# An encoder step in fp32 halves: the seam between the attention part and the MLP is laid out in another order

## The reference

```python
def _layer(x, ...):
    h = _rmsnorm(x, g_mix)
    q_m, k_m, v_m, o_m, i_pre, f_pre, q_a, k_a, v_a = _split_cols(h @ w_in)
    h_til, c1, n1, m1 = _mlstm_chunkwise(qm, km, vm, i_pre + b_igate, f_pre + b_fgate, c0, n0, m0, chunk)
    h_m = jax.nn.sigmoid(o_m) * _rmsnorm(h_til, g_head...)
    o_a = _swa_attention(qb, kb, vb, q_pos, k_pos, attn_sinks)
    x = x + jnp.concatenate([h_m, o_a], axis=-1) @ w_out
    x = x + jnp.square(jax.nn.relu(_rmsnorm(x, g_mlp) @ w_up)) @ w_down
    x = x + jax.nn.sigmoid(_rmsnorm(x, g_ple) @ w_ple_gate) * (p @ w_ple_proj)
```

## Time and profile before

| | us |
|---|---|
| median of 3 runs (lowest, highest) | 2599.46 (2599.33, 2600.07) |
| the profiled execution, its time | 2600.81 |
| its span in the profile | 2599.2 |
| PE busy | 2558.8 |
| DVE busy | 1884.8 |
| ACT busy | 905.1 |
| POOL busy | 78.7 |

### The profile page before, as it was taken

One profiled execution on the slowest core, in us unless ns is written; L12 is line 12 of the kernel. 1 busy time (PEld: TensorE's weight loads), 2 busy tenths in 40 slices (PEclk: granted clock), 3 DMA queues, 4 the chain that ended last, 5 costly groups with the idle time before them and its releaser, 6 DMA issues.

```text
span 2599.2 us, 40780 instructions
## 1 busy us (share of the span) xinstructions
PE 2558.8 (98%) x14143; PEld 2224.1 (86%) x14143; DVE 1884.8 (73%) x3281; ACT 905.1 (35%) x2097; POOL 78.7 (3%) x170
## 2 busy tenths in 40 slices
PE   8999999999999999999999999999999999999999
PEld 6888888878888878999999888989888888888887
DVE  7777777775555568777777788888887887885443
ACT  5333333454444443222222323232332332343322
POOL 0000000000000000000000000000000000000010
PEclk9999999999999999999999999999999999999999
DMA  5112111542232336222222542323342222233223
GB/s 211 58 57 85 56 56 51 178 156 98 105 109 97 112 129 236 65 65 65 65 65 65 196 136 65 97 65 97 121 156 81 65 80 65 81 142 135 86 73 108
DMA packets 163367, 261.86 MB, mean 101 GB/s; under 512 B 11440, under 2 KB 111256, under 8 KB 162520
## 3 DMA queue, kind: packets, MB, share of 16 engines
q1 hardware_dynamic: 160936, 252.29, 28.9%
q0 software_dynamic: 2352, 8.52, 1.0%
HBM read 199.99 MB, written 60.62 MB: 100 GB/s over the span
## 4 chain that ended last, share of the span: by engine, by line
PE 89%; DVE 6%; issue 2%; ACT 1%; DMA 1%; POOL 0%; ACTq 0%; DVEq 0%; SPq 0%; POOLq 0%
PE m_proj L112 12%; PE m_proj L114 12%; PE m_proj L113 12%; PE m_turned L112 6%; PE m_turned L114 6%; PE m_turned L113 6%; PE m_acc L114 5%; PE m_acc L112 5%; PE m_acc L113 5%; PE m_pair L113 4%; PE m_pair L112 4%; PE m_pair L114 4%; PE m_pair L1260 1%; PE m_turned L1268 1%; PE m_acc L1285 1%
## 5 line engine op out<-in xcount | busy, mean ns | idle before, releaser
L2082 ACT ACTIVATE f_up_hi<-f_sums 128x512 fp32r<-128x512 f32 x138 | 85.8, 621 | 507.1 <-DVE f_sums L2365 489.8
L2396 DVE TENSOR_TENSOR f_part<-f_part,m_acc 128x384 f32<-128x384 f32 (+2 forms) x240 | 119.2, 513 | 139.9 <-PE m_acc L114 137.1
L112 PE MATMUL m_proj<-f_down_hi,f_uT_hi 128*128 128x512 f32 x476 | 188.9, 397 | 2.5 <-DVE f_acc L2439 2.5
L114 PE MATMUL m_proj<-f_down_hi,f_uT_lo 128*128 128x512 f32 x476 | 185.6, 390 | 0.0
L112 PE MATMUL m_turned<-f_down_hi,f_uT_hi 128*128 128x512 f32 x472 | 183.9, 390 | 1.6 <-DVE f_acc L2431 0.9
L113 PE MATMUL m_proj<-f_down_lo,f_uT_hi 128*128 128x512 f32 x476 | 185.2, 389 | 0.0
L113 PE MATMUL m_turned<-f_down_lo,f_uT_hi 128*128 128x512 f32 x472 | 184.1, 390 | 0.0
L114 PE MATMUL m_turned<-f_down_hi,f_uT_lo 128*128 128x512 f32 x472 | 183.9, 390 | 0.0
L2439 DVE TENSOR_TENSOR f_acc<-f_acc,m_proj 128x1024 f32<-128x1024 f32 x118 | 143.7, 1218 | 45.4 <-PE m_proj L114 45.2
L2439 DVE TENSOR_TENSOR f_acc<-f_acc,m_turned 128x1024 f32<-128x1024 f32 x131 | 151.5, 1156 | 27.6 <-PE m_turned L114 25.5
L2106 ACT ACTIVATE f_uT_hi<-f_part 128x256 fp32r<-128x256 f32 (+2 forms) x300 | 92.3, 364 | 202.0 <-PE m_turned L114 122.2
(11 more groups left out here) (452 smaller groups left out, 7324.8 us busy)
## 6 DMA issues: line engine op xcount, KB each, us to landing
f_down_raw<-in_w_down SPq DMA_DIRECT2D x96, 512.0 KB, 5.1
f_up_raw<-in_w_up SPq DMA_DIRECT2D x92, 512.0 KB, 5.2
hT_hi_kept<-m_hT_hi SPq DMA_DIRECT2D x17, 512.0 KB, 5.0
hT_lo_kept<-m_hT_lo SPq DMA_DIRECT2D x17, 512.0 KB, 5.8
a_hT_hi<-hT_hi_kept SPq DMA_DIRECT2D x17, 512.0 KB, 3.7
a_hT_lo<-hT_lo_kept SPq DMA_DIRECT2D x17, 512.0 KB, 4.6
m_x<-in_x_prompt SPq DMA_DIRECT2D x16, 512.0 KB, 4.2
a_x_sum<-in_x_prompt SPq DMA_DIRECT2D x16, 512.0 KB, 6.2
```

The source lines that it names most:

```text
L112: eng.matmul(out, lh(k), rh(k), start=f, stop=False)
L114: ins = eng.matmul(out, ll(k), rh(k), start=False, stop=e)
L2082: act.activation(up_hi[:, q], weight(q), ACT.Copy).then_inc(up_hi_made, 1)
L2396: dve.tensor_tensor(part[out][:, 0:w], part[other][:, 0:w], up_ps[bank][:, 0:w], ALU.add).then_inc(combined, 1)
```

## The change

- **SP**: block 0's up weights are loaded behind the stores of round 16's K and V (mark "kept") and not at the end of round 16.
- **DVE and ACT, weights**: the sums and the first low part go into round 16 (mark "split"), three more low parts behind the second softening of round 17, the last three behind the decode tile's shares (mark "shared").
- **Operands**: on DVE the five of a unit (B11, T1, T3, B22, T2) are made as one chain each; unit 0's chain goes ahead of tile 15's second add. Then come unit 0's low T2, the chains of units 1 and 2 and their low T2s, then round 18 of attention (scaling of tile 15, the decode tile's adds), then the nine low parts of T3, T1, B21, then the T4s. ACT has the same order in HI_EARLY, HI_NEXT, HI_LATE, and comes back to attention's round 18 (its copy of tile 15's `hxT`) behind the last T4. The operands have other places in memory (FIRST_PLACE).
- **Decode tile on PE**: its mLSTM heads are turned in round 17 between the halves of the tile 15 product, ACT copies them there, and four of eight chunks of its high product are done ahead of the average. Tile 15's `turn_x` goes behind the third of the seven first up products.
- **PE, every round from 2 to 17**: the second scores go ahead of the wait for the low mixed operand and of `turn_x`.
- **POOL**: unit 2's rows are loaded ahead of tile 15's root.

```diff
@@ -960,7 +960,6 @@
     EARLY = 2
-    FRONT, BACK = 2, 6
@@ -1062,6 +1061,8 @@
                 sp.dma_start(out_v[which][P - rows:P, :], kv[0:rows, slot, KVW:]).then_inc(kept_out, 16)
+            if on_round(r, NT):
+                yield "kept"
             if exists(r - 2):
@@ -1168,8 +1169,9 @@
                 act.activation(mixT_to[:, HEADS:KC, 0:old.n], outT[slot][:, :, 0:old.n], ACT.Copy).then_inc(mix_hi, 1)
-                all_of(act, mix_turned, old.i)
-                act.activation(mixT_to[:, 0:HEADS, 0:old.n], turned[:, 0:HEADS, 0:old.n], ACT.Copy).then_inc(mix_hi, 1)
+                if not on_round(r, NT + 2):
+                    all_of(act, mix_turned, old.i)
+                    act.activation(mixT_hi[:, 0:HEADS, :], turned[:, 0:HEADS, :], ACT.Copy).then_inc(mix_hi, 1)
             if on_round(r, NT + 1):
@@ -1186,6 +1188,8 @@
                 if on_round(r, NT + 1):
+                    all_of(act, mix_turned, NT)
+                    act.activation(mixT_dec[:, 0:HEADS, :], turned[:, 0:HEADS, 0:DEC], ACT.Copy).then_inc(mix_hi, 1)
                     yield "free"
@@ -1195,6 +1199,8 @@
                     act.activation(q_parts[rows, :, b, 0:cur.n], turned[rows, 0:GRP, 0:cur.n], ACT.Copy).then_inc(qk_rounded, 1)
+                if on_round(r, NT):
+                    yield "split"
             if on_round(r, 1):
@@ -1323,8 +1329,13 @@
                     pe.wait_ge(*m.heads_done)
+                if on_round(r, NT + 2):
+                    reached(pe, mix_hi, NT * 2 + 1)
+                    reached(pe, added, (NT - 1) * 2 + 1)
+                    project_last_out(wo_hi, range(HEADS))
                 average(old)
-                turn_heads(old)
+                if not on_round(r, NT + 2):
+                    turn_heads(old)
             if exists(cur.i):
@@ -1333,24 +1344,23 @@
                 project_kv(cur)
+            if exists(mid.i) and not on_round(r, 1):
+                score(mid, 1)
             if on_round(r, NT + 2):
                 all_of(pe, mix_hi, old.i, 2)
-                project_last_out(wo_hi, range(FRONT)).then_inc(o0_ps, 1)
-            elif exists(old.i):
+                project_last_out(wo_hi, range(HEADS, KC)).then_inc(o0_ps, 1)
+                project_last_out(wo_lo, range(1)).then_inc(o0_ps, 1)
+                project_last_out(wo_lo, range(1, KC)).then_inc(o1_ps, 1)
+                yield "out"
+                turn_x(done)
+                yield r
+                return
+            if exists(old.i):
                 all_of(pe, mix_lo, old.i, 2)
...
                 turn_x(done)
-            if exists(mid.i) and not on_round(r, 1):
-                score(mid, 1)
             if on_round(r, 2):
                 pe.wait_ge(wo_lo_made, HALF)
-            if on_round(r, NT + 2):
-                project_last_out(wo_hi, range(FRONT, BACK)).then_inc(o0_ps, 1)
-                project_last_out(wo_hi, range(BACK, KC))
-                project_last_out(wo_lo, range(1)).then_inc(o0_ps, 1)
-                project_last_out(wo_lo, range(1, KC)).then_inc(o1_ps, 1)
-                yield r
-                return
             if exists(old.i):
@@ -1362,6 +1372,9 @@
                 project_out(0, second).then_inc(o0_ps, 1)
+                if on_round(r, NT + 1):
+                    reached(pe, sT_sb, NT * 2 + 1)
+                    turn_heads(mid)
                 all_of(pe, kv_sb, r if exists(r) else NT)
@@ -1375,7 +1388,7 @@
                 else:
-                    reached(pe, sT_sb, mid.i * 2 + 1)
+                    reached(pe, mix_hi, NT * 2 + 1)
                 turn_s(mid, 1)
@@ -1480,8 +1493,6 @@
                 split_mix(old)
-            if on_round(r, NT + 2):
-                yield "mixed"
             if exists(cur.i) and not on_round(r, 0):
@@ -1507,6 +1518,8 @@
                 share(mid, 1)
+                if on_round(r, NT + 1):
+                    yield "shared"
             if exists(cur.i):
@@ -1530,8 +1545,8 @@
-    finished = Finished(scaled=(x_scaled, NT + 1), q_ps=(q_ps, NT + 1), kv_ps=(kv_ps, NT + 1), front_ps=(o0_ps, NT + 1), out_ps=(o1_ps, NT + 1), x_out=(x_out, 16 * (NT + 1)), hxT_out=hxT_out, kept_out=(kept_out, 96),
-                        middle_ps=(o0_ps, NT + 2), back_ps=(o0_ps, NT + 3), mix_ps=(o1_ps, NT), soft=(soft, (NT * 2 + 1) * SOFT + 1))
+    finished = Finished(scaled=(x_scaled, NT + 1), q_ps=(q_ps, NT + 1), kv_ps=(kv_ps, NT + 1), front_ps=(out_done, NT + 1), out_ps=(o1_ps, NT + 1), x_out=(x_out, 16 * (NT + 1)), hxT_out=hxT_out, kept_out=(kept_out, 96),
+                        middle_ps=(o0_ps, NT + 1), back_ps=(o0_ps, NT + 2), mix_ps=(o1_ps, NT), soft=(soft, (NT * 2 + 1) * SOFT + 1))
     return Programs(sync, gpsimd, scalar, tensor, vector), finished
@@ -1559,7 +1574,7 @@
             whole(m)
-            upto(a, NT)
+            upto(a, "kept")
             next(f)
@@ -1575,7 +1590,7 @@
             next(f)
-            upto(a, NT + 2)
+            upto(a, NT + 1)
             next(f)
@@ -1593,6 +1608,8 @@
             whole(m)
+            upto(a, "split")
+            next(f)
             upto(a, "free")
@@ -1611,7 +1628,7 @@
             whole(m)
-            upto(a, NT + 2)
+            upto(a, "out")
             upto(f, "drained")
@@ -1637,11 +1654,13 @@
             whole(m)
+            upto(a, "split")
+            next(f)
             upto(a, "free")
             next(f)
+            upto(a, "shared")
+            next(f)
             upto(a, "idle")
-            next(f)
-            upto(a, "mixed")
             next(f)
@@ -1919,13 +1938,13 @@
         if p == 0:
-            return by_pair(by_unit[:, u, lo, which])
+            return by_pair(by_unit[:, u, lo, FIRST_PLACE[which]])
         return by_pair(by_pass[p][lo][:, which, :, unit_cols(p, u)])
...
             return by_pass[p][lo][:, q, c, :]
-        return by_unit[:, :, lo, q, c, :]
+        return by_unit[:, :, lo, FIRST_PLACE[q], c, :]
@@ -1937,13 +1956,13 @@
-    STAGED_FIRST = [(0, T1), (0, T3), (0, T2), (0, T4), (1, T1), (1, T3), (1, T2), (2, T1), (2, T3), (2, T2), (1, T4), (2, T4)]
-    HI_EARLY = [(0, B11), (0, B22), (0, B21), (0, T2), (0, T3)]
-    HI_BY_STAGE = [(1, B11), (1, B22), (2, B11), (2, B22), (1, T2), (2, T2), (1, T3), (2, T3), (0, T1), (1, T1), (2, T1),
-                   (1, B21), (2, B21), (0, T4), (1, T4), (2, T4)]
-    HI_FIRST = HI_EARLY + HI_BY_STAGE
-    LO_FIRST = [(0, B11), (0, B22), (0, B21), (0, T2), (0, T3), (1, B11), (1, B22), (2, B11), (2, B22), (1, T2), (2, T2), (1, T3), (2, T3),
-                (0, T1), (1, T1), (2, T1), (1, B21), (2, B21), (0, T4), (1, T4), (2, T4)]
+    STAGED_FIRST = [(0, T1), (0, T3), (0, T2), (1, T1), (1, T3), (1, T2), (2, T1), (2, T3), (2, T2), (0, T4), (1, T4), (2, T4)]
+    HI_EARLY = [(0, B11), (0, B22)]
+    HI_NEXT = [(0, T2), (1, B11), (1, B22), (2, B11), (2, B22), (1, T2), (2, T2)]
+    HI_LATE = [(0, T3), (1, T3), (2, T3), (0, T1), (1, T1), (2, T1), (0, B21), (1, B21), (2, B21), (0, T4), (1, T4), (2, T4)]
+    HI_FIRST = HI_EARLY + HI_NEXT + HI_LATE
+    LO_FIRST = [(0, B11), (0, B22), (0, T2), (1, B11), (1, B22), (2, B11), (2, B22), (1, T2), (2, T2)] + HI_LATE
+    FIRST_PLACE = {T3: 0, B11: 1, B22: 2, T2: 3, T1: 4, B21: 5, T4: 6}
@@ -2133,19 +2152,23 @@
-        whole(ready(0, 0))
+        weights = ready(0, 0)
+        next(weights)
+        next(weights)
+        yield
+        whole(weights)
         act.wait_ge(*a.soft)
-        first_hi(*HI_EARLY[0])
-        yield
-        for u, which in HI_EARLY[1:]:
+        for u, which in HI_EARLY:
             first_hi(u, which)
...
         act.wait_ge(*a.front_ps)
-        for u, which in HI_BY_STAGE:
-            if (u, which) == (2, B11):
-                act.wait_ge(*a.middle_ps)
+        for u, which in HI_NEXT:
             first_hi(u, which)
+        act.wait_ge(*a.middle_ps)
+        for u, which in HI_LATE:
+            first_hi(u, which)
+        yield
         for p in PASSES:
@@ -2219,6 +2242,8 @@
             for q, out in enumerate(out_all):
+                if q == 3:
+                    upto(rest, NT + 2)
                 if q == 6:
@@ -2507,35 +2532,37 @@
-        add_weights(0)
-        whole(ready(0, 0))
-        yield
-        first_lo(0, B11)
-        first_stage(0, T1)
-        first_stage(0, T3)
-        yield
-        first_lo(0, B22)
-        first_stage(0, T2)
-        first_lo(0, B21)
-        first_stage(0, T4)
-        first_lo(0, T2)
-        first_lo(0, T3)
-        for u in (1, 2):
-            if u == 2:
-                dve.wait_ge(*a.back_ps)
+        def first_chain(u):
             first_lo(u, B11)
...
             first_stage(u, T2)
-        for u, which in LO_FIRST[9:16]:
+
+        weights = ready(0, 0)
+        add_weights(0)
+        next(weights)
+        yield
+        for _ in range(3):
+            next(weights)
+        yield
+        whole(weights)
+        first_chain(0)
+        yield
+        first_lo(0, T2)
+        first_chain(1)
+        dve.wait_ge(*a.middle_ps)
```

(14 more changed lines are left out.)

## The result

The changed kernel took 2618.37 us (median of 4 runs, 2618.11 to 2618.72), the kernel before, beside it on the same chip, 2599.39 (4 runs, 2597.90 to 2600.07): a ratio of 1.0075 [1.0063, 1.0087], 19.0 us slower.

What follows compares the result with a forecast made beforehand. PE, busy 98% of the span, was taken as the bound. Block 1's later start of 14.65 us plus 1.5 for the clock gave +16.1, added to the median 2599.46: 2615.6 us, range 2608 to 2621.

Steps and rivals of the forecast that it cites:

- The deciding step: SP, round 18: held until ACT's row copy at 986.4, so second up weights land at 1007.7; block 1 14.65 us later.
- the queue: DMA, before block 1: POOL's four pass 1 loads delay the second up weights by 4.0 us, of 0 to 5.1.
- sign that the queues slow each other: Tile 16's 128 KB store, issued at 989.13 with POOL's loads close behind, took 10.2 us; read as queues slowing each other.
- Rival (a): Same wait of SP, but POOL's loads cost nothing: +12.2 us, 2611.6; chance 0.20.
- Rival (b): Same wait, with 5.1 for the queue, 3.0 for the clock, 1.5 for down weights: +20.2, 2619.7; chance 0.12.
- The clock term: PE, start of block 1: restarts at the lower clock after over 10 us idle, losing 1.5 us, of 1.1 to 3.0.
- The steady rounds: PE, every round: second scores moved ahead of the low mixed operand's wait and turn_x; 0, between -0.5 and +0.5 us.
- The lead at the first product: PE, round 18: first up product starts near 974 to 975 instead of 979.67, 5 us ahead.
- The full clock at 948: PE, round 17: scores cut the 1.89 us gap to 0.9, so PE stays at full clock.
- The reason given for the lost lead: ACT takes P1 behind the T4s, so PE stands from 983.3 to 986.9; DVE's chain is only 1.8 to 2.1 ahead.
- rival (d): First operands ready 5 to 5.6 us sooner and lead kept, with P1 and row copy on time: 2594.0; chance 0.04.
- Rival (c): No change: second weights land before DVE reaches them near 990.9; block 1 starts some 2.1 earlier, 2597.3; chance 0.07.

Runs made afterwards that it cites:

- Experiment 1: Changed kernel, but SP passes its mark "loads" ahead of the store of tile 15's rows in round 18; 2598.74 us, ratio 1.0000.
- experiment 2: Kernel before, with one added SP wait for the 21st high operand ahead of the first up weights' stores; 2616.43 us, ratio 1.0068.
- experiment 3: Changed kernel, but POOL's four loads for pass 1 wait until the second up weights have landed; 2613.31 us, ratio 1.0057.
- experiment 4: Experiment 1 with the second scores of rounds 2 to 16 behind turn_x again, round 17's still moved; 2598.42 us, ratio 0.9999.
- experiment 6: Kernel before with only the early load, sums and first parts of the first up weights in round 16; 2598.57 us, ratio 0.9996.
- Experiment 7: Experiment 5 with ACT's three high T4s moved behind its copy of tile 15's rows and P1; 2596.80 us, ratio 0.9993.
- experiment 5: Experiment 1 with ACT making the third and fourth high up weights ahead of the decode tile's heads; 2598.18 us, ratio 0.9997.
- experiment 8: Experiment 7 with unit 0's high T2 ahead of the square of tile 15 on ACT; 2596.88 us, ratio 0.9993.
- experiment 9: Experiment 7's kernel run again, unchanged, for more runs; 2597.92 us, ratio 0.9995.

## Why the prediction was right, and where it was off

**The deciding step** held, with its place and its cause: SP's program stands at tile 15's rows, behind it the first weights' stores and the second weights' loads. The store came at 986.69 (foreseen: the copy ends at 986.4; it did at 986.66), the load landed at 1009.7 (1007.7). Experiment 1 takes the wait away and the loss goes; experiment 2 makes it alone and the loss comes. Together they leave no room for another cause of more than a microsecond or two. (Experiment 2's spans differ by 14.2 and not 17.7; its sums start 3.4 sooner than after's, which accounts for it.)

**The size** was 1.6 us short of the spans' difference (+16.1 for +17.7): 1.7 from one term of the sum, the queue, 0.4 ahead of the seam and 0.5 the other way from the clock, and the last two are within what traces differ by. Against the medians the forecast of 2615.6 was 2.8 short of 2618.37. The other 1.2 are the base: I added a difference to before's profiled execution to a median that lies 1.35 below it. That execution holds the 1.7 us of the clock at 948, so against the 66.81 without that fall the seam lost 18.0.

I took 4.0 for the queue, of 0 to 5.1, the upper end being POOL's bytes at the rate of the earlier trace rows. It was 5.7 as after stands to before (23.0 - 17.3), and 6.1 with POOL's loads taken away (experiment 3), over the upper end that I had worked out. The rate of the best microsecond was no bound. From the end of the copy to the first sum, after moved 8.27 MB in 23.1 us, a mean of 358 GB/s, and experiment 3 5.90 MB in 17.0, 348 GB/s. By 358 the 2.1 MB are 5.9 us. The difference is 2.37 MB: 2.10 of POOL's queue and 0.26 more of SP's own.

The prediction's sign that the queues slow each other, the 10.2 us of tile 16's store of 128 KB, was misread. Six loads of acc tiles stood right ahead of it on SP's own queue:

```profile
981.08 7.57 SPq L1970 DMA_DIRECT2D f_acc<-x_after_mixers  x6
```

In after the same store, issued at 1007.56 behind the same six loads, took as long, and from 1007.5 to 1017.7 POOL's queue moved nothing:

```profile
x_after_mixers<-a_x_sum SPq DMA_DIRECT2D x1, 128.0 KB, 10.1
```

In experiment 1, where it is issued 6 us after the last of the six loads and POOL's loads come 1.8 us behind it, it took 4.2. So the choice of 4.0 rested in part on a wrong sign, and that it came near is partly luck; experiment 3 is what shows that POOL's loads cost the weights time.

Rival (a), no cost of the queue, falls with experiment 3. Rival (b), 2619.7, was nearer to the measured time (1.3 over) than the forecast (2.8 under). Its queue term was nearer, but 3.0 for the clock is not borne out, and PE has no further gap behind 1013.19 that before lacks, so the down weights cost 0.
The Trainium skill (DMA: Bandwidth & Descriptors, Queues, rings and completion order) has each DMA engine take turns between the queues by packets; the prediction said that by this rule the charge lies near the upper end, and experiment 3 agrees with 6.1 us.

**The clock term** was 1.5 of 1.1 to 3.0, and what stands behind the first sum grew by 1.0. Whether that is under the range can't be told: the three kernels with a late block 1 have 1607.05 to 1608.15 there, the other eight 1605.30 to 1607.16, and their means differ by 1.4. PE ran at 1.2 GHz for 5.4 us behind the restart; at full loss that would be 2.7. Part of these microseconds DVE's low parts set the pace anyway, as the prediction said of 0.5 of them. The growth in experiment 2 is 0.9.

**The steady rounds** were given 0 (within 0.5); the ruler's start moved 0.4, less than traces differ by, and experiment 4 shows no worth in the moved scores.

**The lead at the first product** came as foreseen (974.40 for "974 to 975"), and so did the new stall before the decode product (966.32 for 966.0, 1.90 us for 2.2), tile 15's add (964.25 in 963.7 to 964.4), the first sums without a wait, and P1's gap (3.33 us, 987.19 for 986.9). The full clock at 948 with a gap of 0.97 was right too, but the gain was put down to the change by mistake: in experiments 2 and 6 the clock stayed full with the gap still at 1.89. Against experiment 2 on the ruler the first product came 3.9 us sooner (49.49 for 53.42) and not 5.3.

**The reason given for the lost lead** was half right. The prediction put it on ACT, which takes P1 behind the T4s, and named DVE's chain, "1.8 to 2.1 ahead", second. Experiment 7 moves P1 out of the way: the gap goes and block 1 starts no sooner. DVE's chain sets it: 2.1 us ahead of the earlier trace rows in after, 2.4 on the ruler in experiment 1. Of both, 1.7 is the fallen clock of before's trace; 0.7 is what is left of the 3.9 on PE. It follows that rival (d) failed in its mechanism as well: with P1 and the rows on time, nothing like 5 us would have been kept. Rival (c)'s number was "block 1 starts some 2.1 earlier, 2597.3". Experiment 1, where the second weights are hidden, is its case: 2.44 on the ruler against before's trace, 0.7 without its fall, 2598.74 in time. The change without SP's wait is rival (c), and within the measurement no change.

**What stays open.** The 0.5 to 1 us by which what stands behind the first sum differs between the kernels with an early block 1 (1605.3 to 1607.2) isn't settled; it is as large as the differences that experiments 5 to 9 were after, and one trace of each can't tell it. Why SP's own queue moved 0.26 MB more in after's stretch isn't settled either, nor what made the clock fall at 948 in one execution and not in two others with the same gap. Of the parts of the change, the early weights and the second scores were measured by themselves; the order of the operands and the decode tile's work on PE were not.

## What to carry to other kernels

When operations of one stage are moved past those of another, look at every queue's program, the DMA queues' above all: a store that waits for a copy holds each load written behind it, and a copy of 1 us that nobody on PE needed for long cost 16 us through SP. A gap of PE taken away at one place is worth only as much as the chain that feeds the next stage moves; here 3.9 us of lead on PE were 0.7 us on DVE, and the early weights alone gave 1.2. Where a difference is 0.1% or less, the distance between two fixed instructions of the trace repeats better than the time (0.13 us in two traces of experiment 7's kernel). But look at the granted clock in that distance first: two traces of the kernel before differ in it by 1.7 us, for a fall that one of them has. A sum worked out from one trace takes over whatever that execution happened to do.

## What the runs showed of the hardware beyond that

- Loads of 2.1 MB on POOL's queue delayed the loads already queued on SP's by 6.1 us, over the 5.1 that the bytes take at 414 GB/s. The mean rate over the whole stretch was 358 GB/s with them and 348 without.
- A store of 128 KB took 10.2 and 10.1 us behind six loads of 512 KB on its own queue (before, after), in the second case with nothing moving on POOL's queue, and 4.2 when it was issued 6 us after the last of them (experiment 1).
- The length of one gap didn't decide PE's clock. With 1.89 us ahead of `turn_x` it fell at 948 in before and stayed full in experiments 2 and 6. With the stall of 1.90 in round 18 it fell at 967 in after and at 966 in experiment 1, for some 3.4 us, and stayed full in experiment 3 (1.90) and experiment 4 (1.93). The gap of about 1.0 ahead of `turn_x` left it full in all eight traces that have it. The fall doesn't come at once: behind the gap of 3.33 the first products at 987.19 ran at full pace (0.33 us each), and those from 987.96 at 0.50.
- Seven programs whose seams differ by up to 3.6 us on the ruler (before, experiments 1 and 4 to 8; 1.7 of it the clock in before's trace) had medians from 2596.8 to 2599.4; single runs of the kernel before spread from 2597.1 to 2601.3.
